# Feed-forward products of 512 columns with their own gate signal, and weight splits moved amid the activation steps

## The reference

```
h = rms_norm(x, g)
x = x + 0.5 * (silu(h @ w_gate) * (h @ w_up)) @ w_down      # d_ff = 2816
```

## Time and profile before

| | us |
|---|---|
| median of 3 runs | 1549.43 |
| lowest, highest | 1548.29, 1549.53 |
| profiled execution, own time | 1547.91 |
| its span | 1545.6 |

### The profile page before, as it was taken

The page is one execution under the profiler, slowest core; times in us unless marked ns, Lnnn a source line. Parts: engine busy times, 40 slices in busy tenths (PEclk is TensorE's granted clock), DMA queues, the critical chain, the costliest instruction groups (busy, mean ns, idle before and its releaser), DMA issues.

```text
span 1545.6 us, 29393 instructions
## 1 busy us (share of the span) xinstructions
PE 1510.1 (98%) x11792; PEld 1394.9 (90%) x11792; DVE 790.1 (51%) x1054; ACT 763.1 (49%) x1051; POOL 511.6 (33%) x201
## 2 busy tenths in 40 slices
PE   7999999999999999999999999999999999999997
PEld 6999988988999999999988999999999887899996
DVE  4444456567444454444555634445444489844433
ACT  5444465336444454444576634445434578543433
POOL 2434300000434336444362344434343300044342
PEclk9999999999999999999999999999999999999999
DMA  6544532134554535545443445444545452354542
GB/s 258 204 183 184 192 135 83 62 120 150 204 183 184 193 133 204 203 173 194 179 148 118 157 180 199 176 189 168 199 167 201 166 196 104 110 202 165 196 175 90
DMA packets 48087, 259.95 MB, mean 168 GB/s; under 512 B 5376, under 2 KB 5632, under 8 KB 27296
## 3 DMA queue, kind: packets, MB, share of 16 engines
q1 hardware_dynamic: 47664, 258.68, 45.5%
q10 hardware_dynamic: 288, 0.34, 0.1%
q0 software_dynamic: 80, 0.14, 0.0%
HBM read 258.08 MB, written 1.05 MB: 168 GB/s over the span
## 4 chain that ended last, share of the span: by engine, by line
PE 87%; DVE 6%; ACT 4%; issue 1%; POOL 1%; DMA 1%; SPq 0%; DVEq 0%; ACTq 0%; POOLq 0%
PE banks L367 81%; DVE arena L2446 2%; DVE gu_lo L347 1%; ACT gu_hi L338 1%; DMA raw_gu<-units_gu 1%; PE banks L1300 1%; ACT arena L402 1%; ACT h_hi L385 1%; PE banks L1309 1%; DVE x L474 1%; PE banks L1255 0%; DVE h_lo L418 0%; PE banks L2106 0%; ACT arena L2351 0%; ACT arena L2324 0%
## 5 line engine op out<-in xcount | busy, mean ns | idle before, releaser
L360 POOL TENSOR_TENSOR dn_lo<-raw_dn,dn_hi 128x1024 fp32r<-128x1024 f32 x138 | 476.7, 3455 | 887.0 <-ACT dn_hi L343 876.9
L367 PE MATMUL banks<-h_hi,gu_hi 128*128 128x256 f32 x2256 | 642.8, 285 | 7.3 <-DVE h_lo L418 7.0
L367 PE MATMUL banks<-h_lo,gu_hi 128*128 128x256 f32 x2256 | 638.8, 283 | 0.0
L367 PE MATMUL banks<-h_hi,gu_lo 128*128 128x256 f32 x2256 | 638.7, 283 | 0.0
L347 DVE TENSOR_TENSOR gu_lo<-raw_gu,gu_hi 128x2048 fp32r<-128x2048 f32 x161 | 370.5, 2301 | 203.2 <-ACT gu_hi L338 203.2
L367 PEld LDWEIGHTS banks<-h_hi,gu_hi 128*128 128x128 f32 x2256 | 432.6, 192 | 15.6 <-issue 5.9
L367 PEld LDWEIGHTS banks<-h_lo,gu_hi 128*128 128x128 f32 x2256 | 432.8, 192 | 5.1 <-issue 0.5
L367 PEld LDWEIGHTS banks<-h_hi,gu_lo 128*128 128x128 f32 x2256 | 432.6, 192 | 0.0
L338 ACT CAST gu_hi<-raw_gu 128x2048 fp32r<-128x2048 f32 x161 | 306.7, 1905 | 42.5 <-DMA raw_gu<-units_gu 28.1
L482 ACT ACTIVATE silu<-silu 128x256 f32<-128x256 f32 x132 | 55.2, 418 | 511.3 <-DVE silu L490 511.2
L367 PE MATMUL banks<-dn_hi,act_hi 128*128 128x512 f32 x528 | 207.1, 392 | 0.0
(11 more groups left out here) (342 smaller groups left out, 1273.0 us busy)
## 6 DMA issues: line engine op xcount, KB each, us to landing
raw_gu<-units_gu SPq DMA_DIRECT2D x161, 1024.0 KB, 5.9
raw_dn<-units_dn SPq DMA_DIRECT2D x162, 512.0 KB, 3.5
x<-x_in SPq DMA_DIRECT2D x2, 512.0 KB, 5.5
raw_gu<-units_gu SPq DMA_DIRECT2D x2, 512.0 KB, 8.2
out<-x SPq DMA_DIRECT2D x1, 1024.0 KB, 3.9
cst<-constants SPq DMA_DIRECT2D x1, 688.0 KB, 12.3
lora<-low_rank SPq DMA_DIRECT2D x1, 512.0 KB, 13.4
arena<-final_gain SPq DMA_DIRECT2D x1, 512.0 KB, 4.1
```

Of the source, the lines that this page charges most:

```text
L360: nc.gpsimd.tensor_tensor(dn_lo[:, p, 0:n], raw_dn[:, p, 0:n], dn_hi[:, p, 0:n].bitcast(F32), ALU.subtract).then_inc(dn_lo_ready, 1)
L367: ins = nc.tensor.matmul(out, a, b, start=first and i == 0, stop=last and i == 2)
```

## The change

1. `h_hi` and `h_lo` become two views of one tile `h_both` [128, 8, 2, 256], in which the 256 high and the 256 low columns of a block stand side by side.
2. In units 2 to 20 of a stage (2 to 19 in the last stage) the high weights are multiplied with both in one matmul of 512 columns that fills a bank, and the low weights with the high input in one of 256 columns into its first half. The second half holds hi x lo and is added later. Gate and up have a bank each: banks `2p` and `2p+1`. Units 0, 1 and 21 keep the three products.
3. `gate_summed` tells that the gate side is summed, after half of `ffn_up`; before, gate and up were told together by `gu_used`.
4. ScalarE copies the second half of each bank to SBUF (`lo_half`), and VectorE adds it to the first.
5. In those units `hi_gu` of unit u+2 comes before the act_hi copy of unit u, and `lo_gu` before act_lo; before, they came behind.
6. The row of rstd is summed in bank 7. The first pair of each stage, and the last but one on TensorE, are written out and not in the loop.

The core of the diff:

```
-        h_hi, h_lo = sb("h_hi", [P, KD, T], F32R), sb("h_lo", [P, KD, T], F32R)
+        h_both = sb("h_both", [P, KD, 2, T], F32R)
+        h_hi, h_lo = h_both[:, :, 0, :], h_both[:, :, 1, :]
...
+        lo_half = arena[:, 16, 0:4 * T].rearrange("p (u i t) -> p u i t", u=2, i=2)
...
-                ins = nc.tensor.matmul(banks[:, 2, t * P:(t + 1) * P], const("ones"), rstd_diag[:, t, :], start=True, stop=True)
+                ins = nc.tensor.matmul(banks[:, 7, t * P:(t + 1) * P], const("ones"), rstd_diag[:, t, :], start=True, stop=True)
...
+        FIRST_BOTH, LAST_BOTH = 2, FFN_UNITS - 2
+        def both_before(f):
+            return f // FFN_UNITS * (LAST_BOTH - FIRST_BOTH + 1) - FIRST_BOTH
...
+        def ffn_act(act, pair, p, f, ahead, both=None):
             hi_dn(act, pair, p)
+            if both is not None:
+                act.wait_ge(gate_summed, f + 1)
+                nc.scalar.copy(lo_half[:, p, 0, :], banks[:, 2 * p, T:2 * T]).then_inc(lo_copied, 1)
             act.wait_ge(gate_ready, f + 1)
             nc.scalar.activation(silu[:, p, :], silu[:, p, :], ACT.Silu).then_inc(silu_ready, 1)
+            if both is not None:
+                act.wait_ge(gu_used, 2 * pair + p + 1)
+                nc.scalar.copy(lo_half[:, p, 1, :], banks[:, 2 * p + 1, T:2 * T]).then_inc(lo_copied, 1)
+                hi_gu(act, pair + 1, p)
             act.wait_ge(act_ready, f + 1)
             nc.scalar.copy(act_hi[:, p, :], act32[:, p, :]).then_inc(act_hi_ready, 1)
-            if ahead:
+            if ahead and both is None:
                 hi_gu(act, pair + 1, p)
...
+        def ffn_dve(dve, pair, p, f, ahead, both=None):
+            if both is None:
+                dve.wait_ge(gate_summed, f + 1)
+                nc.vector.tensor_tensor(silu[:, p, :], banks[:, 2 * p, 0:T], rstd_row, ALU.mult).then_inc(gate_ready, 1)
+                dve.wait_ge(gu_used, 2 * pair + p + 1)
+                dve.wait_ge(silu_ready, f + 1)
+                nc.vector.tensor_tensor(act32[:, p, :], silu[:, p, :], banks[:, 2 * p + 1, 0:T],
+                                        ALU.mult).then_inc(act_ready, 1)
+            else:
+                dve.wait_ge(lo_copied, 2 * both + 1)
+                nc.vector.tensor_tensor(silu[:, p, :], banks[:, 2 * p, 0:T], lo_half[:, p, 0, :],
+                                        ALU.add).then_inc(halves_added, 1)
+                dve.wait_ge(halves_added, 2 * both + 1)
+                nc.vector.tensor_tensor(silu[:, p, :], silu[:, p, :], rstd_row, ALU.mult).then_inc(gate_ready, 1)
+                dve.wait_ge(lo_copied, 2 * both + 2)
+                nc.vector.tensor_tensor(act32[:, p, :], banks[:, 2 * p + 1, 0:T], lo_half[:, p, 1, :],
+                                        ALU.add).then_inc(halves_added, 1)
+                dve.wait_ge(silu_ready, f + 1)
+                dve.wait_ge(halves_added, 2 * both + 2)
+                nc.vector.tensor_tensor(act32[:, p, :], silu[:, p, :], act32[:, p, :], ALU.mult).then_inc(act_ready, 1)
+                lo_gu(dve, pair + 1, p)
             dve.wait_ge(act_hi_ready, f + 1)
             nc.vector.tensor_tensor(act_lo[:, p, :], act32[:, p, :], act_hi[:, p, :].bitcast(F32),
                                     ALU.subtract).then_inc(act_lo_ready, 1)
-            if ahead:
+            if ahead and both is None:
                 lo_gu(dve, pair + 1, p)
...
                     w = slice((side * KD + k) * P, (side * KD + k + 1) * P)
+                    if both:
+                        nc.tensor.matmul(banks[:, 2 * p + side, :], gu_hi[:, p, w],
+                                         h_both[:, k, :, :].rearrange("p i t -> p (i t)"), start=k == 0, stop=False)
+                        ins = nc.tensor.matmul(banks[:, 2 * p + side, 0:T], gu_lo[:, p, w], h_hi[:, k, :], start=False,
+                                               stop=k == KD - 1)
+                    else:
+                        ins = three_products(banks[:, 2 * p + side, 0:T],
+                                             (gu_hi[:, p, w], gu_lo[:, p, w]), (h_hi[:, k, :], h_lo[:, k, :]),
+                                             k == 0, k == KD - 1)
+                ins.then_inc((gate_summed, gu_used)[side], 1)
```

More of the change, by code:

```diff
@@ L312, in build @@
         gu_used, dn_used = sem("gu_used"), sem("dn_used")
-        gate_ready = sem("gate_ready")
+        gate_ready, gate_summed, lo_copied, halves_added = (sem(n) for n in ("gate_ready", "gate_summed", "lo_copied",
+                                                                             "halves_added"))
         silu_ready, act_ready = sem("silu_ready"), sem("act_ready")
@@ L452, in rstd_row_act @@
             act.wait_ge(row_summed, ffn_index(s) + 1)
-            nc.scalar.copy(rstd_row, banks[:, 2, 0:T]).then_inc(row_ready, 1)
+            nc.scalar.copy(rstd_row, banks[:, 7, 0:T]).then_inc(row_ready, 1)
         def ffn_index(s):
@@ L496, in ffn_dve, with ffn_up @@
                                     ALU.subtract).then_inc(act_lo_ready, 1)
-            if ahead:
+            if ahead and both is None:
                 lo_gu(dve, pair + 1, p)
-        def ffn_up(pe, pair, p, f, norm=None):
+        def ffn_up(pe, pair, p, f, norm=None, both=True):
             if norm == 0:
@@ L558, in ffn_all_act @@
             rstd_row_act(act, s)
[L559 to L566, removed]
+            n = both_before(f)
+            ffn_act(act, b, 0, f, True)
+            ffn_act(act, b, 1, f + 1, True)
+            with act.Fori(1, HALF - 1) as i:
+                ffn_act(act, b + i, 0, f + 2 * i, True, n + 2 * i)
+                ffn_act(act, b + i, 1, f + 2 * i + 1, True, n + 2 * i + 1)
             i = HALF - 1
-            ffn_act(act, b + i, 0, f + 2 * i, s + 1 < len(stages))
+            ffn_act(act, b + i, 0, f + 2 * i, s + 1 < len(stages), n + 2 * i if s + 1 < len(stages) else None)
             ffn_act(act, b + i, 1, f + 2 * i + 1, False)
@@ L593, in ffn_all_dve @@
             dve.wait_ge(row_ready, ffn_index(s) + 1)
[L594 to L601, removed]
+            n = both_before(f)
+            ffn_dve(dve, b, 0, f, True)
+            ffn_dve(dve, b, 1, f + 1, True)
+            with dve.Fori(1, HALF - 1) as i:
+                ffn_dve(dve, b + i, 0, f + 2 * i, True, n + 2 * i)
+                ffn_dve(dve, b + i, 1, f + 2 * i + 1, True, n + 2 * i + 1)
             i = HALF - 1
-            ffn_dve(dve, b + i, 0, f + 2 * i, s + 1 < len(stages))
+            ffn_dve(dve, b + i, 0, f + 2 * i, s + 1 < len(stages), n + 2 * i if s + 1 < len(stages) else None)
             ffn_dve(dve, b + i, 1, f + 2 * i + 1, False)
@@ L624, in ffn_all_pe @@
             gained_pe(pe, s)
-            ffn_up(pe, b, 0, f, s)
+            ffn_up(pe, b, 0, f, s, both=False)
             rstd_row_pe(pe, s)
-            ffn_up(pe, b, 1, f + 1)
+            ffn_up(pe, b, 1, f + 1, both=False)
             ffn_down(pe, b, 0, f, True, False)
-            with pe.Fori(0, HALF - 1) as i:
+            with pe.Fori(0, HALF - 2) as i:
                 ffn_up(pe, b + 1 + i, 0, f + 2 + 2 * i)
@@ L634, in ffn_all_pe @@
                 ffn_down(pe, b + 1 + i, 0, f + 2 + 2 * i, False, False)
+            i = HALF - 2
+            ffn_up(pe, b + 1 + i, 0, f + 2 + 2 * i, both=s + 1 < len(stages))
+            ffn_down(pe, b + i, 1, f + 1 + 2 * i, False, False)
+            ffn_up(pe, b + 1 + i, 1, f + 3 + 2 * i, both=False)
+            ffn_down(pe, b + 1 + i, 0, f + 2 + 2 * i, False, False)
             ffn_down(pe, b + HALF - 1, 1, f + FFN_UNITS - 1, False, True)
@@ L1803, in outputs @@
                 k = 4 * g + 2 * i
-                done(cp(h_hi[:, k:k + 2, :].rearrange("p h t -> p (h t)"), banks[:, k, :]), ("hi", g, i))
+                done(cp(h_hi[:, k:k + 2, :], banks[:, k, :].rearrange("p (h t) -> p h t", h=2)), ("hi", g, i))
             for t in range(2):
```

15 lines of the change are left out of this document (2 added, 13 removed).

## The result

| | before | after |
|---|---|---|
| median of 20 runs each, us | 1549.66 | 1551.71 |
| lowest to highest | 1547.56 to 1551.62 | 1549.27 to 1558.87 |
| profiled execution's span | 1545.6 | 1549.0 |

The ratio is 1.0017, 95% interval 1.001 to 1.0024: two microseconds slower, inside the 0.2% that the prediction calls no change, where 7 us faster was forecast. The time lies inside the range given (1529 to 1552), but the change went the other way.

The account below looks back on a forecast made before the run. TensorE, 98% busy, was taken as the bound: number of matmuls times their step. Saving 22 us and stalls of 15 us gave -7, so 1549.43 became 1542.4 us; range 1529 to 1552, the forecast's own 1538 to 1547.

Parts of the forecast that it names:

- The saving: Gate and up products on TensorE: a merged pair costs 0.2275 instead of 0.2396 us, 22 us less over 113 units.
- Rival 3: TensorE matmuls: the 0.013 surcharge goes with columns or weights, so merging saves nothing; 15 us slower, 1564; chance 0.06.
- The stalls: Start of each feed-forward stage: TensorE waits for act_lo before unit 2's down product, together 15 us.
- the distance: At a stage's start: from TensorE's start of unit 2's up product to ScalarE's start of unit 3's high copy; 1.11 to 4.19.
- the forecast's rule: At a stage's start, the stall before unit 2's down product is the distance plus 0.42 us.
- Who goes first: When VectorE's gu_lo ends, GpSimd's waiting dn_lo goes before act_lo, which comes 2.2 us later.
- rival 1: After gu_lo, act_lo goes before GpSimd's dn_lo: stalls only 4 us, 1531 us; chance 0.22.
- mirror image: Earlier trace at 789.25: VectorE's gu_lo, waiting during dn_lo, was served before GpSimd's next instruction; gu_lo ended at 792.10.
- The ring: Feed-forward units: the chain from one act_lo end to the next takes 8.2 us, just fitting TensorE's 8.31.
- Rival 2: Feed-forward units: the ring is longer than TensorE's unit, so every unit after the start waits; 1564 at 8.53; chance 0.15.

Follow-up runs that it names:

- e3: The kernel after, with each side's eight products of 512 columns first and then its eight of 256: 1547.4 us, ratio 0.9985 to before.
- e4: The kernel after, with the low weights also multiplied with both inputs, so that all products have 512 columns: 1717.9 us, one run.
- e8: The kernel after, with GpSimd making only the first 512 of 1024 columns of the down weights' low part (dn_lo): 1537.9 us, one run.
- e1: The kernel after, with both weight splits back in their old places, behind act_hi and act_lo: 1592.4 us, ratio 1.0286 to before.
- e5: The kernel after, with the three old products and no copies or adds, but both weight splits still moved ahead: 1555.5 us, ratio 1.0049 to before.
- e2: The kernel after, with only the low part of the next weights back behind act_lo, the high copy staying early: 1536.2 us, ratio 0.9919 to before.
- e7: The kernel after, with e2 and e3 together (low part behind act_lo, products grouped by width): 1527.0 us, ratio 0.9855 to before.
- e10: The kernel of e7, with SyncE issuing raw_gu of a unit before raw_dn of the one before, as in e6: 1533.6 us, ratio 0.9887 to before.
- e6: The kernel after, with SyncE issuing raw_gu of a unit before raw_dn of the one before: 1543.4 us, ratio 0.9965 to before.

## Why the prediction was wrong

- **The saving: the step that failed.** It is the term of 22 us: "The steps at the changes of size fit the size of the earlier matmul alone", and so "0.194 us" a unit, 22 us. Measured: 0.11 a unit and 12.4 in all; this alone turns the forecast's -7 into +2.6. The two changes of size in the earlier trace rows are rounded to 0.01 and lie 48 matmuls apart; the effect is 0.005 for the two changes of a pair, half of what they can resolve, and 32 of them come in a unit. The forecast's own sum, 15 on and 22 off, stood on this difference of small steps. The bound of "19 to 24" was too narrow: it counted the rounding of the two steps, not the unmeasured change between them. e3 restores 8.30 by order alone and e4 shows no surcharge without a change of width. Rival 3's sign to look for ("pairs of 0.355 or more") was almost met, but its mechanism, a surcharge by columns or weights, was not at work.
- **The stalls: right in mechanism, place and order, somewhat large.** One stretch before the down product of unit 2 in each stage, released by act_lo, L364 3.56 and act_lo 2.58 long, as written. Idle 10.9 where 15 was summed. The first stage makes 2.0 of it: raw weights of unit 3 landed 7.1 after their issue before and 5.4 after, so the distance was 1.6 and not 3.36, the stall 1.76 and not 3.8. Why that DMA was faster is not shown; the stall is smaller by luck. In the last stage the distance was 1.59 for 1.79, and the slower unit itself grants 0.16 more: 1.74 for 2.2. Put into the forecast's rule with that 0.16, the distances measured after (1.61, 1.28, 1.76, 1.91, 1.59, the third stage left out) give 1.87, 1.54, 2.02, 2.17 and 1.85, each 0.11 or 0.12 above the stall measured: the rule was right, the distances had moved. The forecast's own bounds (19 to 24 saved, 12 to 18 stalled) add up to 1537.4 and 1548.4, a little wider than the 1538 to 1547 given. The third stage has two stalls of 2.05 together for the 2.5 taken.
- **Who goes first (rival 1): settled as forecast.** From one mirror image; now act_lo has a median of 2617 ns over 132 instructions, and e8 shortens it to 1517 by shortening dn_lo alone. The Trainium skill, page "SBUF — State Buffer", section "Who interferes with whom", calls the shared pair of ports an exclusive lock; the traces agree, and add that the engine that already waits gets it before the next instruction of the one that held it.
- **The ring: right.** Summed to 8.2; act_lo started at 1380.08 and next at 1388.22 and 1396.40, 8.14 and 8.18. It fits TensorE's 8.39 with more room than thought. Rival 2 did not occur here, but it does in the order of before (e1, 8.82), and there it made the change 41 us slower: the forecast took up the moved splits only as a cost and never asked what the new work would cost without them.
- **The clock: not foreseen.** One fall of 1.7 behind a stall and two of 3.0 together in the second stage. The forecast has no term for the clock. Whether a stall brings a fall on is not shown: e3 has one behind its first stall, e5 none behind its four, and most falls lie elsewhere. No run shows why the falls in the second stage come: e2 has none there, e5 and e7 one, e10 two, and the idle stretches of TensorE there are alike (busy 11.4 to 11.6 of 14 us in all).
- **The sum.** With 12.4 for 22, 11.5 for 15 and 4.7 of clock for nothing, the step from -7 to +3.8 is there; measured in the profiles +3.4, in the medians +2.05.

## What to carry to other kernels

A change that trades many small steps for fewer must be priced in the order in which the steps will run: alternating two matmul widths cost 0.005 us a pair here, nearly half of what merging them saved, and grouping them by width gave it back. Before moving a step ahead of another, write down the ring that it closes with every engine that shares a memory port, and try the half of the move that does not lie in it: here neither part moved gives 1592, both 1552, ScalarE's high part alone 1536. A stall at the start of each stage can be as large as a gain in all its units; the rows of one stage's start deserve the same walk as the steady state.

## What the hardware showed that was not expected

- **Change of width.** 512 behind 512 is 0.227 and 256 behind 256 is 0.120; alternating, a pair is 0.3525 and not 0.347.
- **Order of service at the shared port.** A VectorE instruction of 0.42 us with two SBUF inputs took 2.17 or 2.58 when GpSimd had asked while VectorE's gu_lo still ran; with a PSUM input it took 0.42 in the same place (1372.70).
- **What lies behind a stall.** The first step of a down product after an idle stretch is 0.33 or 0.34 in place of 0.23 (887.28 less 886.94), and in one of seven the clock stood at 1.2 GHz for some 3 us behind it. Kernels with stalls showed a median granted clock of 0.993 to 0.9955 over their spans (the kernel after, e3, e5), e2 and e7 without them 0.9965 and 0.9975; but e6 and e10, with hardly any, have 0.994 and 0.995, so a link between stalls and the clock is open.
